# Gate one-hots for sixteen tokens at a time, and key places summed by halving

## The reference

```
q = (xb @ w_q).reshape(128, 8, 2, 128)              # 8 heads, two halves each
s = einsum('bhpd,hpkd->bhpk', q, sub_keys)          # 128 sub-keys in each half
sv, si = top_k(s, 16)
cand = sv[:, :, 0, :, None] + sv[:, :, 1, None, :]  # 16 x 16 sums
cv, ci = top_k(cand, 16)
i1 = take_along_axis(si[:, :, 0], ci // 16);  i2 = take_along_axis(si[:, :, 1], ci % 16)
idx = i1 * 128 + i2                                 # an expert of 16384
gate = softmax(cv)
act = gelu(einsum('bhkd,bd->bhk', u_emb[idx], xb))
out = einsum('bhk,bhkd->bd', gate * act, v_emb[idx])
```

## Time and profile before

| | |
|---|---|
| three runs | 2018.89, 2018.05, 2012.18 us (median 2018.05) |
| profiled execution | 2016.21 us |
| its span, first to last instruction | 2014.5 us |
| PE busy | 1926.0 us (96%) |
| DVE busy | 1462.6 us (73%) |
| ACT, POOL busy | 751.0 us, 738.8 us (37% each) |
| mean DMA rate | 223 GB/s |
| granted clock of PE | 0.981 of full speed |

### The profile page before, as it was taken

The page is one execution under the profiler, slowest core; times in us unless marked ns, Lnnn a source line. Parts: engine busy times, 40 slices in busy tenths (PEclk is TensorE's granted clock), DMA queues, the critical chain, the costliest instruction groups (busy, mean ns, idle before and its releaser), DMA issues.

```text
span 2014.5 us, 35532 instructions
## 1 busy us (share of the span) xinstructions
PE 1926.0 (96%) x14267; PEld 1758.4 (87%) x14267; DVE 1462.6 (73%) x2696; ACT 751.0 (37%) x953; POOL 738.8 (37%) x600
## 2 busy tenths in 40 slices
PE   9998987888999999999999999998899999999997
PEld 8998976767459999988888888888899999999997
DVE  6616664775247778878887997885698788888887
ACT  6334543443032133445444545543223332233323
POOL 8235737560023101322322241221488544333440
PEclk9999988999999999999999999999999999999999
DMA  6212210020231135677888797779999999999993
GB/s 204 64 45 76 66 40 2 9 92 12 71 142 59 68 132 193 237 275 276 330 326 295 274 366 268 287 282 341 356 367 362 386 364 362 360 365 368 358 336 124
DMA packets 179180, 450.11 MB, mean 223 GB/s; under 512 B 15729, under 2 KB 92273, under 8 KB 168817
## 3 DMA queue, kind: packets, MB, share of 16 engines
q1 hardware_dynamic: 125472, 240.77, 34.5%
q0 software_dynamic: 42496, 151.03, 20.3%
q10 hardware_dynamic: 11088, 56.63, 6.9%
HBM read 383.26 MB, written 65.07 MB: 223 GB/s over the span
## 4 chain that ended last, share of the span: by engine, by line
PE 77%; DVE 9%; POOL 4%; DMA 3%; ACT 3%; issue 3%; SPq 1%; ACTq 0%; DVEq 0%; POOLq 0%
PE bank L2028 27%; PE bank L1943 23%; PE bank L1897 5%; PE bank L1360 5%; PE bank L1849 3%; DMA v_raw<-in_pv 2%; PE bank L1952 2%; PE bank L1380 1%; DMA sca<-in_pu_rows,pick 1%; PE bank L1919 1%; DVE u_lo L2602 1%; DVE sca L2608 1%; DVE pre L2166 1%; SPq L595 1%; PE bank L1570 1%
## 5 line engine op out<-in xcount | busy, mean ns | idle before, releaser
L1943 PE MATMUL bank<-xhi,u_hi 128*128 128x448 f32 x1008 | 380.0, 377 | 5.2 <-ACT actb L1236 5.2
L1943 PE MATMUL bank<-xhi,u_lo 128*128 128x448 f32 x1008 | 369.8, 367 | 0.0
L1943 PE MATMUL bank<-xlo,u_hi 128*128 128x448 f32 x1008 | 368.7, 366 | 0.0
L842 POOL DMA_INDIRECT sca<-in_pu_rows,pick x128 | 173.1, 1352 | 527.9 <-DVE sdot L2608 414.1
L2028 PE MATMUL bank<-w_hi,v_hi 128*128 128x416 f32 x1024 | 358.3, 350 | 6.1 <-DVE w_lo L2861 5.4
L2028 PE MATMUL bank<-w_lo,v_hi 128*128 128x416 f32 x1024 | 357.8, 349 | 0.0
L2028 PE MATMUL bank<-w_hi,v_lo 128*128 128x416 f32 x1024 | 357.7, 349 | 0.0
L1289 ACT ACTIVATE v_hi<-v_raw 128x4096 fp32r<-128x4096 f32 x32 | 115.9, 3621 | 394.1 <-PE bank L2028 355.7
L2867 DVE TENSOR_TENSOR v_lo<-v_raw,v_hi 128x4096 fp32r<-128x4096 f32 x32 | 141.6, 4425 | 95.7 <-ACT v_hi L1289 95.7
L2602 DVE TENSOR_TENSOR u_lo<-u_raw,u_hi 128x2048 fp32r<-128x2048 f32 x64 | 146.5, 2290 | 86.8 <-ACT u_hi L1208 82.5
L1943 PEld LDWEIGHTS bank<-xhi,u_hi 128*128 128x128 f32 x1008 | 189.7, 188 | 19.6 <-issue 5.6
(11 more groups left out here) (698 smaller groups left out, 3728.7 us busy)
## 6 DMA issues: line engine op xcount, KB each, us to landing
u_raw<-in_pu SPq DMA_DIRECT2D x64, 1024.0 KB, 5.1
v_raw<-in_pv SPq DMA_DIRECT2D x128, 512.0 KB, 8.6
act_scratch<-actb ACTq DMA_DIRECT2D x64, 448.0 KB, 6.1
wts<-act_scratch SPq DMA_DIRECT2D x32, 896.0 KB, 6.9
gate_scratch<-gst ACTq DMA_DIRECT2D x13, 2048.0 KB, 9.0
gring<-gate_scratch SPq DMA_DIRECT2D x32, 832.0 KB, 13.4
wring<-in_w_q SPq DMA_DIRECT2D x4, 2048.0 KB, 8.9
wp_raw<-in_w_in SPq DMA_DIRECT2D x7, 1024.0 KB, 5.4
```

Source lines behind the costliest of these rows:

```text
L842: pool.indirect_dma_start(rows_u[s % RING], None, pu_rows[:, :], bass.IndirectOffsetOnAxis(pick[:, s:s + 1], 0)).then_inc(s_row[s % RING], 16)
L1943: ins = mm(bank[b][:, 0:DS], lhsT, rhs[:, 0:DS], **on)
```

## The change

Three buffers change size and place. `hot_b` grows from 8 to 16 pairs of tokens (eight quads), `hot_a` from two quads to four, `hot_e` from 4 to 8 pairs. `hot_b` and `hot_a` move into the bytes of `xq_b` and `wq_hi_a` (the operands of the query projection, which is over by then); a filler keeps all other buffers where they were. PE's part changes only in its slot numbers.

In `one_hots` the two comparisons are made for four quads at once, in every second group, and the product for two quads at once, in every group. The waits on `gmat_done` follow: the comparisons at quad q wait for q - 4 finished quads (q - 2 before), the product at q for q - 2 (q - 1 before, at each quad). `hots_ready` rises by two after each product. In `sum_keys` the one reduction becomes four additions over 8, 4, 2 and 1 of the 16 elements, the first three in place in 16 bits.

```
-        hot_b = sb("hot_b", [128, 8, 128, 2], f16, scope=first)
-        hot_a = sb("hot_a", [128, 2, 2, 2, 128, 2], f16, scope=first)
-        hot_e = sb("hot_e", [128, 4, 128, 2], f16, scope=first)
+        hot_e = sb("hot_e", [128, 8, 128, 2], f16, scope=first)
+        sb("gap_hot", [128, 1536], scope=first)
...
+        hots = ExitStack()
+        hot_b = sb("hot_b", [128, 16, 128, 2], f16, scope=hots)
+        hot_a = sb("hot_a", [128, 4, 2, 2, 128, 2], f16, scope=hots)
+        hots.close()
...
-                        ins = mm(bank[5 + k % 2][:, 128 * j:128 * j + 128], hot_b[:, 2 * (k % 4) + j // 2, :, j % 2],
-                                 hot_a[:, k % 2, j // 2, part, :, j % 2], start=part == 0, stop=part == 1)
+                        ins = mm(bank[5 + k % 2][:, 128 * j:128 * j + 128], hot_b[:, 2 * (k % 8) + j // 2, :, j % 2],
+                                 hot_a[:, k % 4, j // 2, part, :, j % 2], start=part == 0, stop=part == 1)
...
-                    s = 2 * (quad % 4)
-                    if k % 2 == 0:
...
-                        if quad >= 4:
-                            dve.wait_ge(S("gmat_done"), quad - 2)
-                        TT(hot_b[:, s:s + 4, :, :], every, both[1], ALU.is_equal)
+                    s = 2 * (quad % 8)
+                    if k % 4 == 0:
...
+                        if quad >= 8:
+                            dve.wait_ge(S("gmat_done"), quad - 4)
+                        TT(hot_b[:, s:s + 8, :, :], every, both[1], ALU.is_equal)
                   if quad:
                       dve.wait_ge(S("hots_ready"), quad)
                   link(TT(hot_e[:, :, :, :], every, both[0], ALU.is_equal))
-                    if quad >= 2:
-                        dve.wait_ge(S("gmat_done"), quad - 1)
-                    rows_e = hot_e[:, 2 * (k % 2):2 * (k % 2) + 2, :, :]
-                    TT(hot_a[:, quad % 2, :, :, :, :], rows_e.unsqueeze(2).to_broadcast([128, 2, 2, 128, 2]),
-                       hk_g[:, 2 * k:2 * k + 2, :, :].unsqueeze(3).to_broadcast([128, 2, 2, 128, 2]), ALU.mult
-                       ).then_inc(S("hots_ready"), 1)
+                    if k % 2 == 0:
+                        if quad >= 4:
+                            dve.wait_ge(S("gmat_done"), quad - 2)
+                        rows_e = hot_e[:, 2 * (k % 4):2 * (k % 4) + 4, :, :]
+                        two = hot_a[:, quad % 4:quad % 4 + 2, :, :, :, :].rearrange("p q r a n j -> p (q r) a n j")
+                        TT(two, rows_e.unsqueeze(2).to_broadcast([128, 4, 2, 128, 2]),
+                           hk_g[:, 2 * k:2 * k + 4, :, :].unsqueeze(3).to_broadcast([128, 4, 2, 128, 2]), ALU.mult
+                           ).then_inc(S("hots_ready"), 2)
...
-                link(dve.tensor_reduce(isel[0:n, :, :].rearrange("p a (k r) -> p (a k) r", r=2),
-                                       hot[0:n, :].rearrange("p (k j r) -> p k r j", k=128, j=16), AX.X, ALU.add))
+                places = hot[0:n, :].rearrange("p (k j r) -> p k j r", k=128, j=16)
+                for half in (8, 4, 2):
+                    link(TT(places[:, :, 0:half, :], places[:, :, 0:half, :], places[:, :, half:2 * half, :], ALU.add))
+                link(TT(isel[0:n, :, :].rearrange("p a (k r) -> p (a k) r", r=2), places[:, :, 0, :], places[:, :, 1, :], ALU.add))
```

More of the change, by code:

```diff
@@ L2664, in one_hots @@
                     quad = t0 // 4 + k
-                    s = 2 * (quad % 4)
-                    if k % 2 == 0:
-                        both = [hk_ab[:, a, 4 * k:4 * k + 8].rearrange("p (r j) -> p r j", j=2).unsqueeze(2)
-                                .to_broadcast([128, 4, 128, 2]) for a in range(2)]
-                        every = lanes[:, :, :].unsqueeze(1).to_broadcast([128, 4, 128, 2])
-                        if quad >= 4:
-                            dve.wait_ge(S("gmat_done"), quad - 2)
-                        TT(hot_b[:, s:s + 4, :, :], every, both[1], ALU.is_equal)
+                    s = 2 * (quad % 8)
+                    if k % 4 == 0:
+                        both = [hk_ab[:, a, 4 * k:4 * k + 16].rearrange("p (r j) -> p r j", j=2).unsqueeze(2)
+                                .to_broadcast([128, 8, 128, 2]) for a in range(2)]
+                        every = lanes[:, :, :].unsqueeze(1).to_broadcast([128, 8, 128, 2])
+                        if quad >= 8:
+                            dve.wait_ge(S("gmat_done"), quad - 4)
+                        TT(hot_b[:, s:s + 8, :, :], every, both[1], ALU.is_equal)
                         if quad:
```

## The result

The changed kernel took 2034.43 us in the median of four runs (2030.67 to 2039.26) against 2015.12 us (2011.13 to 2018.89): a ratio of 1.010, interval 1.0073 to 1.0128. Forecast were 2020.9 us and no change that can be told, in a range up to 2027. The time went up by 15 to 26 us.

A forecast was written before the change was run, and what follows sets the result against it. PE bounds the kernel, so the end moves only where PE waits for DVE. Terms -2.4 + 3.2 + 1.6 + 0.4 + 0.1 = +2.9 us give 2020.9 us from the median 2018.05; range 2013 to 2027.

The forecast's parts named there:

- a sign that was forecast: DVE's idle time before `u_lo` would be larger, if the forecast is right.
- Part (1): Groups 10 and 11: later comparisons still leave `u_lo` in time, waits behind the sum go at three places, -2.4 us.
- The clock, a rival: Waits of 3.1 us at both groups 14 and last tile's start lower PE's clock, 3 x 2.4 us more; chance 0.15.
- (2): Group 14, two places: two comparisons and a two-quad product come before PE's quad, 1.6 us later each, +3.2 us.
- (3): Start of the last tile: the larger one-hots come behind `few_places`, so PE's quad starts later, +1.6 us.
- Part (4): Starts of the first three tiles: first one-hots 0.2 us late, +0.4 us; second and third tie, +0.1 us.
- Part (6): The turn to the sums: moves as a whole with PE, new buffer bytes bring no new wait, taken as 0.
- a sign against it: The turn's two PE idle times differing from 10.6 us by more than 2 would show the forecast wrong.

The follow-up runs named there:

- the delay alone: Kernel before with comparison `hot_e` made twice more, 1.4 us of delay, in front of both groups 14: 2020.94 us, ratio 1.0022.
- the shifted comparisons: Changed kernel with the sixteen-token comparisons made one group later, in odd groups 1 to 13, eight-token ones in groups 0 and 15: 2016.34 us, ratio 0.9999.

## Why the prediction was wrong

The frame held in the main: PE bounds, the durations were right to 0.01 us, and 16 us less work on DVE brought no time back (DVE's idle time before `u_lo` in the gated groups went from 66 to 100 us, a sign that was forecast). That the change can move the end "only where PE waits for DVE" was too narrow: 5.8 us came from the clock behind the waits and 2.3 us from slower steps without any wait. By its own steps:

1. **Part (1), group 10, is the step that failed.** It said that the comparisons end later there, and tested only whether `u_lo` was in time for the next group ("covered"). The first quad of group 10 stands behind the same instructions, and PE wants it before `u_lo`. Its one-hots were ready at about 947.6 us against a wish of 947.4 before; 1.6 us later is simply 1.6 us lost. That is +4.8 us at three places, priced at nothing; the table has 1.59 each. That the place had no slack stood in the part's own rows: the 0.83 us laid to the sum were counted over six steps, of which the one to group 10 already took 5.64 us in place of 5.43; group 11 alone had lost 0.62. The rest of the part held: the waits behind the sums went. In the first tile the product was ready at 959.7 and PE came for it at 962.05, 2.3 us later, of which 1.6 us are PE's own lateness; the 0.7 us left are those of the forecast. Only the gain was over-priced by those 0.2 us: 1.7 us in the table in place of 2.4.
2. **The clock, a rival with a chance of 0.15, came true at all three places** that it named. Its price was 3 x 2.4 us; measured are 1.6, 2.7 and 1.5, together 5.8. The argument against it, that 3.1 us lie nearer to 2.6 than to 5.2, compared with a single case in another stage. The run with the delay alone shows the same without the change. The size of a wait does not decide it: a wait of 1.9 us was followed by a low clock with both buffers moved, and one of 3.1 us by none (quad 90 of the sixteen-token kernel with one-hots a group ahead, next step 5.43 us); at that same quad a wait of 2.04 us was followed by a low clock with the shifted comparisons and one of 2.05 us by none with comparisons for eight tokens. The Trainium skill, "TensorE: Matmul & The Clock Gate", Part 1, calls the window by which the clock is set free-running, so that it would matter how a stall falls on it. These waits fit that; no run here shows the window itself.
3. **Parts (2) and (3) held**: +1.4, +1.9 and +1.7 us against 1.6 each. Part (4) was short by 0.6: the starts of the first three tiles cost 0.3, 0.6 and 0.2 us, 1.1 together against 0.5.
4. **Part (6), "no new wait" for the new bytes**, was right, but the new places (of `hot_a`, or `hot_e`) slow PE's plain steps by 0.5%, +2.3 us. No row of before could show it. The turn, taken as 0, moved by more than the 2 us that the prediction named as a sign against it: PE's two idle times fell from 10.6 to 6.4 us and the turn took 6.2 us less. The sums took 4.1 us more, and neither goes with the change; that the two nearly cancel is luck for the forecast's zero.

The forecast's +2.9 us, plus 4.8 for group 10, 5.8 for the clock, 2.3 for the place, 0.6 for part (4), 0.7 for the smaller gain behind the sums and 0.2 for groups 14 and the last tile, is 17.3; the gated groups with the first quad measured 17.2. Group 10 could have been read from the trace of before; with it alone the sum would have been +7.7 us, slower by more than 0.3%.

## What to carry to other kernels

Where an engine with time to spare feeds the one that bounds, ask of every instruction that grows which result stands behind it and how long before its deadline it comes; list all consumers of a delayed point, the nearest first, not only the next one in the text. Merging two small steps into one delays the first half by the second. A stall of 2 to 3.5 us on TensorE may cost 1.2 to 2.8 us more in clock, or nothing; price it as a chance, not by its length. And moving work ahead of a chain of fetched rows may only move the wait, as it did here, to the next point that cannot be made ahead.

## What the runs showed of the hardware

- The granted clock fell to half (its 1.2 GHz level) at waits of PE of 1.9, 2.0, 2.4, 2.7, 2.9 to 3.5 and above 5 us, and stayed full at others of 1.6 to 2.1 us and at one of 3.1 us; a fall cost 1.2 to 2.8 us in the step behind. Busy time of PE by stretches of 4 us (busy us, clock, DMA share, GB/s), first with both buffers moved, behind a wait of 1.9 us, then with comparisons for eight tokens, behind one of 2.1 us:

```profile
1168.00:1172.00 4.00, 2.42 (x12) 1.00 0.89 340
1172.00:1176.00 4.00, 3.70 (x17) 0.58 0.73 259
```

```profile
1336.00:1340.00 4.00, 2.32 (x12) 1.00 1.02 434
1340.00:1344.00 4.00, 3.63 (x24) 1.00 0.46 141
```

- The same matmuls go by 5.463 us a step or by 5.433, with the bytes in which `hot_a` lies, in all thirteen profiles: 5.46 in the six with the new place, 5.43 in the seven with the old one. In the same six `hot_e` lies at the start of the old bytes, and in none of the seven, so no run parts the two buffers. Why a place slows matmuls most of which read neither stays open.
